# Late stage of a diffusion-transformer layer: four PSUM places for the out tiles, the first tiles interleaved by k, the sums of squares added behind the norm's steps

## What is computed

```python
merged = sigmoid(g_dn) * (y_dn @ w_branch_dn) + sigmoid(g_at) * (y_at @ w_branch_attn)
x = x + g_a_x * (merged @ w_out)
h = modulate(rms_norm(x, norm_ffn), sh_f_x, sc_f_x)
u = dwconv_centred(h @ ffn_up, ffn_conv) + ffn_conv_b      # 1024 -> 2 * 2816 channels
x = x + g_f_x * ((silu(u_gate) * u_val) @ ffn_down)
```

## Time and profile before

| | |
|---|---|
| median of 3 runs | 2613.94 us (2612.71 to 2618.61) |
| the profiled execution: its time | 2618.86 us |
| its span, first to last instruction | 2617.1 us |
| instructions in the profile | 40,299 |
| `late_stage` from its first out tile to its third up tile | 1773.8 to 1899.6 us |

### The profile page before, as it was taken

One profiled execution on the slowest core, in us unless ns is written; L12 is line 12 of the kernel. 1 busy time (PEld: TensorE's weight loads), 2 busy tenths in 40 slices (PEclk: granted clock), 3 DMA queues, 4 the chain that ended last, 5 costly groups with the idle time before them and its releaser, 6 DMA issues. The chain is left out here.

```text
span 2617.1 us, 40299 instructions
## 1 busy us (share of the span) xinstructions
PE 2504.8 (96%) x16246; PEld 2088.3 (80%) x16246; DVE 1393.0 (53%) x2110; ACT 811.8 (31%) x1745; POOL 858.4 (33%) x580
## 2 busy tenths in 40 slices
PE   5999999999999999999999989999899999997999
PEld 4768887887888888888888877887688888886887
DVE  6783665213456565565656564256865555555342
ACT  4222554101264554635454463101211111112010
POOL 1443652332324132323324131335433333322121
PEclk9999999999899999999999999999999999998999
DMA  7231322222000010101001011224411111113442
GB/s 271 72 81 53 122 109 90 97 73 81 17 18 25 18 33 9 34 9 42 25 18 33 2 42 57 97 97 126 158 57 49 49 49 49 49 36 102 140 129 90
DMA packets 52646, 177.01 MB, mean 68 GB/s; under 512 B 5360, under 2 KB 14960, under 8 KB 51184
## 3 DMA queue, kind: packets, MB, share of 16 engines
q1 hardware_dynamic: 50160, 170.24, 20.0%
q10 hardware_dynamic: 2304, 4.20, 0.4%
HBM read 148.20 MB, written 20.97 MB: 65 GB/s over the span
## 5 line engine op out<-in xcount | busy, mean ns | idle before, releaser
L201 PE MATMUL late_ps<-h_hi,late_w_hi 128*128 128x512 f32 x784 | 306.4, 391 | 5.8 <-ACTq L127 3.2
L203 PE MATMUL late_ps<-h_hi,late_w_lo 128*128 128x512 f32 x784 | 306.1, 390 | 0.0
L202 PE MATMUL late_ps<-h_lo,late_w_hi 128*128 128x512 f32 x784 | 306.0, 390 | 0.0
L1403 PE MATMUL late_ps<-h_hi,dn_w_hi 128*128 128x512 f32 (+1 forms) x640 | 248.2, 388 | 5.6 <-issue 5.6
L1403 PE MATMUL late_ps<-h_lo,dn_w_hi 128*128 128x512 f32 (+1 forms) x640 | 252.2, 394 | 0.0
L1403 PE MATMUL late_ps<-h_hi,dn_w_lo 128*128 128x512 f32 (+1 forms) x640 | 249.9, 390 | 0.0
L184 POOL CAST late_w_hi<-late_w_raw 128x1024 fp32r<-128x1024 f32 x76 | 79.2, 1042 | 505.9 <-issue 376.2
L191 POOL TENSOR_TENSOR late_w_lo<-late_w_raw,late_w_hi 128x1024 fp32r<-128x1024 f32 x76 | 204.0, 2685 | 6.1
L2444 DVE SCALAR_TENSOR_TENSOR ffn_u<-ffn_pad,vectors,ffn_u 128x1024 f32<-128x1024 f32 x88 | 194.5, 2210 | 3.1
L201 PEld LDWEIGHTS late_ps<-h_hi,late_w_hi 128*128 128x128 f32 x784 | 147.7, 188 | 37.3 <-issue 6.7
L202 PEld LDWEIGHTS late_ps<-h_lo,late_w_hi 128*128 128x128 f32 x784 | 147.6, 188 | 30.8 <-issue 0.2
(11 more groups left out here) (360 smaller groups left out, 6027.3 us busy)
## 6 DMA issues: line engine op xcount, KB each, us to landing
late_w_raw<-in_w_up SPq DMA_DIRECT2D x44, 512.0 KB, 3.5
down_w_raw<-in_w_down SPq DMA_DIRECT2D x32, 704.0 KB, 4.3
late_w_ada<-in_w_ada SPq DMA_DIRECT2D x8, 2048.0 KB, 8.4
dn_w_raw<-in_w_dn SPq DMA_DIRECT2D x32, 512.0 KB, 3.9
w_ada<-in_w_ada SPq DMA_DIRECT2D x8, 1024.0 KB, 11.1
at_w_raw<-in_w_mg_at SPq DMA_DIRECT2D x16, 512.0 KB, 4.0
late_w_raw<-in_w_mg_dn SPq DMA_DIRECT2D x16, 512.0 KB, 3.7
late_w_raw<-in_w_out SPq DMA_DIRECT2D x16, 512.0 KB, 3.8
```

The source lines that it names most:

```text
L201: pe.matmul(out, self.hi[j][:, k, :], xh, start=(k == 0), stop=False)
L202: pe.matmul(out, self.hi[j][:, k, :], xl, start=False, stop=False)
L203: mm = pe.matmul(out, self.lo[j][:, k, :], xh, start=False, stop=(k == self.kt - 1))
L1403: mm = pe.matmul(bank[at_bank(s)][:, 0:n], wt[:, k, :], x[:, k, t0:t0 + n], start=(rest == 0), stop=(rest == GROUP_MM - 1))
```

## The change

Four things change in `late_stage`.

1. Out tiles use the four halves of `ps[0]` and `ps[1]`, and tile q waits for the residual of tile q - 4 (`x1_made(q - 3)`).
2. Out tiles 0 and 1 are interleaved: k = 0 to 6 of tile 0, k = 0 to 6 of tile 1, then k = 7 of tile 0, k = 7 of tile 1. All k-steps of both wait for `merged_lo` of their k.
3. The second token half of the first two up tiles is interleaved by k: for each k, three matmuls of tile 0 and three of tile 1. The wait for the last residual is taken once, ahead of the loop.
4. The adding of the squares leaves `residual(q)` and becomes `added(q)`. For q up to 9 it stands behind the next tile's residual; for q = 10 to 13 behind the two `scaled` and two `low` steps of that turn; for q = 14 and 15 where it was.

No instruction is added or removed, and no size changes.

```diff
--- before.py
+++ after.py
@@ -2188,7 +2188,7 @@
 
         def x1_place(q):
 
-            return ps[0][:, half(q % 2)]
+            return ps[q % 4 // 2][:, half(q % 2)]
 
         with nc.Block() as block:
             @block.sync
@@ -2253,13 +2253,27 @@
                     pe.matmul(ps[3][:, half(b)], mats[:, C_ONE, :], rstd[:, half(b)], start=True, stop=True).then_inc(ss_done, 1)
 
                 sig_ready.wait(pe, KT)
-                for q in range(2 * KT):
+
+                def out_part(q, k0, k1):
+
                     i = LATE_OUT + q
-                    pe.wait_ge(w.split, i + 1)
-                    x1_made.wait(pe, q - 1)
-                    mm = w.product(pe, x1_place(q), i % 2, m_hi, m_lo, q // KT * HALF, HALF,
-                                   parts=m_lo_made if q == 0 else None)
-                    mm.then_inc(w.used.sem, 1)
+                    if k0 == 0:
+                        pe.wait_ge(w.split, i + 1)
+                        x1_made.wait(pe, q - 3)
+                    tk, o = half(q // KT), x1_place(q)
+                    for k in range(k0, k1):
+                        if q < 2:
+                            pe.wait_ge(m_lo_made, k + 1)
+                        pe.matmul(o, w.hi[i % 2][:, k, :], m_hi[:, k, tk], start=(k == 0), stop=False)
+                        pe.matmul(o, w.hi[i % 2][:, k, :], m_lo[:, k, tk], start=False, stop=False)
+                        mm = pe.matmul(o, w.lo[i % 2][:, k, :], m_hi[:, k, tk], start=False, stop=(k == KT - 1))
+                    if k1 == KT:
+                        mm.then_inc(w.used.sem, 1)
+                for k0, k1 in ((0, KT - 1), (KT - 1, KT)):
+                    for q in range(2):
+                        out_part(q, k0, k1)
+                for q in range(2, 2 * KT):
+                    out_part(q, 0, KT)
                     if q == KT + 1:
                         squares(0)
 
@@ -2273,15 +2287,16 @@
                     up_half(t, 0)
                     if t == 0:
                         squares(1)
-                for t in range(2):
-                    for k in range(KT):
-                        h_lo_made.wait(pe, KT + k + 1)
-                        x1_made.wait(pe, 2 * KT)
+                x1_made.wait(pe, 2 * KT)
+                for k in range(KT):
+                    h_lo_made.wait(pe, KT + k + 1)
+                    for t in range(2):
                         o = ps[t][:, half(1)]
                         pe.matmul(o, w.hi[t][:, k, :], h_hi[:, k, half(1)], start=(k == 0), stop=False)
                         pe.matmul(o, w.hi[t][:, k, :], h_lo[:, k, half(1)], start=False, stop=False)
                         mm = pe.matmul(o, w.lo[t][:, k, :], h_hi[:, k, half(1)], start=False, stop=(k == KT - 1))
-                    mm.then_inc(w.used.sem, 1)
+                        if k == KT - 1:
+                            mm.then_inc(w.used.sem, 1)
                 pe.wait_ge(std_made, 2)
 
                 def up_tile(t, place):
@@ -2382,6 +2397,10 @@
                     dve.wait_ge(x_res_in[q % 2], q // 2 * 16 + 16)
                     dve.scalar_tensor_tensor(out=x1[:, t, half(b)], in0=x1_place(q), scalar=core.gate_mix[:, t:t + 1],
                                              in1=x_in[:, q % 2, :], op0=ALU.mult, op1=ALU.add).then_inc(x1_made.sem, 1)
+
+                def added(q):
+
+                    t, b = q % KT, q // KT
                     sq_made.wait(dve, q + 1)
                     acc = rstd[:, half(b)]
                     if t == 0:
@@ -2410,6 +2429,9 @@
                                              op1=ALU.subtract).then_inc(h_lo_made.sem, 1)
                 for q in range(KT + 2):
                     residual(q)
+                    if q:
+                        added(q - 1)
+                added(KT + 1)
                 root(0)
                 for q in range(KT + 2, 2 * KT):
                     residual(q)
@@ -2417,6 +2439,7 @@
                         scaled(0, k)
                     for k in steps_of(q):
                         low(0, k)
+                    added(q)
                 root(1)
                 scaled(1, 0)
                 for k in range(KT):
```

## The result

The changed kernel takes 2620.58 us (median of 22 runs, 2617.32 to 2626.89) beside 2616.01 us of the kernel before on the same chips: 1.0018 times the time of before, 95% interval 1.0013 to 1.0024. By that ratio it is 4.7 us slower, where the forecast was 1.6 us slower. The time lies 1.1 us above the forecast's range (2610.7 to 2619.5), though its 0.18% are within the 0.2% that the forecast called no change; the upper end of the interval is not. The forecast counted from the 2613.94 us of three runs of the kernel before, and its median is 2.1 us higher over more runs, so of the 5.1 us between forecast and result 2.1 are the starting point, and 3.0 are what the change cost beyond its forecast.

What follows compares the result with a forecast made beforehand. TensorE, busy 96% of the span, was taken as the bound, with only 11.7 us of late-stage waits to win. Terms +0.5 + 2.1 - 1.0 = +1.6 us on 2613.94 gave 2615.5 us, range 2610.7 to 2619.5.

Steps and rivals of the forecast that it cites:

- Part 1: Out tiles 0 and 1 interleaved: `merged_lo` wait becomes about 3.2 us for POOL; tile 2 starts 0.5 to 0.6 us later.
- about 0.1 for restarting: At tile 2's start behind the wait for POOL: PE's restart adds about 0.1 us.
- Parts 2 and 3: Four PSUM places, and DVE from residual 9 on: one 6.0 us wait, first up tile starts +0.5 us, at about 1871.2.
- the waits for squares: DVE's turns q = 10 to 13: four waits of 0.70 us for the square go, -2.8 us.
- POOL's split: Ahead of residual 14: all six weight splits now lie before it and hold DVE, +2.4 us.
- The clock: Behind the 6.0 us wait ahead of the first up tile: PE falls to 1.2 GHz, +2.1 us, bounds 0 and 5.1.
- Part 4: Up tiles interleaved: small waits give way to about 3 us for POOL; up tile 2 starts 1.0 us earlier.
- from there to residual 10: Addition of square 8 behind residual 9 lengthens POOL's `lo` and delays the addition of 9: +0.3 us.
- DVE loses all that it gained: Rival, DVE's turns ahead of the first up tile: +3.3 + 2.1 - 1.0 = +4.4 us, 2618.3 us; chance 0.09.

Runs made afterwards that it cites:

- the experiment with short `lo`: Changed kernel with POOL's `lo` for out tiles 11 to 15 and up tiles 0 and 1 cut to one of 8 blocks: 2610.97 us, ratio to before 0.9984.
- the fillers: Changed kernel plus matmuls of no use in PE's three long waits (12, 26 and 12): 2616.01 us, ratio to before 1.0003.

## Why the prediction was off

**Part 1** was right in its working: the wait for POOL was forecast at about 3.2 us and is 3.0, tile 2 starts 0.43 us later where 0.5 to 0.6 was forecast. **The step that failed** is the next one: the sum took "about 0.1 for restarting" and no clock. The clock fell there, 1.4 us in the profile.

**Parts 2 and 3** named the right mechanism and had two of their terms wrong in size. There is one wait ahead of the first up tile, forecast 6.0 and measured 6.7 us, and the experiment with short `lo` shows that the bound was named rightly. That tile's start was forecast at 97.4 us after out tile 0 and is 99.4. Most of the 2.0 is part 1's fall of the clock. The rest lies in the turns of DVE: residual 10 to the end of residual 14 takes 32.5 us, before 32.0, where -2.8 for the waits for squares and +2.4 for POOL's split had given -0.4. Both terms missed the same way: the squares moved with two places make these turns 2.45 us shorter (29.5), and four places then make them 3.0 longer. The moved additions are on two SBUF inputs as well, and two of them now meet POOL's `lo` in the changed kernel and take 2.88 us each, where before the four took 1.3 to 1.6.

**The clock** behind the long wait fell as forecast; its price was 1.3 us in place of 2.1.

**Part 4** was right in its order: from the first to the third up tile it takes 29.1 us, 28.9 before; with 1.3 for the clock in between that is -1.1, forecast -1.0. Again the sum left out the fall behind the wait: 1.7 us behind up tile 2's start.

The whole difference of the two profiles, beside the terms of the forecast (clock: 24 matmuls behind the wait, beside the same 24 of the kernel before; its step behind a wait is in them):

| term | forecast, us | measured, us |
|---|---|---|
| start of tile 2 | +0.6 | +0.43 |
| clock behind tile 2's start | 0 | +1.44 |
| from there to residual 10 | +0.3 | +0.07 |
| residual 10 to the end of residual 14 | -2.8 + 2.4 | +0.54 |
| clock behind the first up tile's start | +2.1 | +1.31 |
| first to third up tile without the clock | -1.0 | -1.08 |
| clock behind the third up tile's start | 0 | +1.70 |
| sum | +1.6 | +4.41 |

So the term "The clock" was mis-sized: taken once, at 2.1 us, where it stands three times, 1.44 + 1.31 + 1.70 = 4.45 in the profile; the fillers gave 4.0 of it back. That is 2.35 us of the 2.8 that the sum missed, the turns of DVE are 0.9, and the small terms give 0.5 back. The rival "DVE loses all that it gained" has the measured number, +4.4, by luck: it puts 2.8 us more on DVE and one fall of the clock, where DVE took 0.9 more and the clock 2.35.

The forecast priced the wait of 6 us and never asked the same of the two new waits for POOL. It also said that the kernel before shows nothing between 2.7 and 13.1 us of idling. That was misread. The profile of before has a wait of 3.15 us ahead of the matmul at 1619.78, and the clock fell behind it (waits from 1500 on, then the stretch behind the wait, columns as in the earlier trace rows):

```profile
PE late_ps L201 <- ACTq L127: 3.2, 1, 3.2
```

```profile
1620.00:1623.50 3.50, 3.50 (x10) 2.69 (x10) 0.00 (x0) 3.15 (x3) 3.14 (x2) 0.52 0.57 181
```

It has one of 5.56 us too, ahead of 627.7, and the granted clock is 0.52 from 627 to 634. Either would have asked for a fall behind the new waits as a term of the sum.

What the fall of the clock hangs on stays open. From out tile 0 to the down projection, in all ten profiles, the clock fell behind each wait of 3.0 us (6 of 6) and each of 6.7 us or more (3 of 3), and behind one of the ten waits of 2.4 to 2.7 us. Ahead of out tile 0, in the same profiles, the length of a wait does not decide alone: a wait of 3.15 us is followed by a fall in four of the ten profiles (clock 1.00 from 1618 to 1622 in the changed kernel), and a wait of 2.4 us near 445, behind small matmuls of 128 columns, goes with a fall in all ten. So a wait in one place is followed by a fall in some executions and not in others, and each kernel has one profile. By the Trainium skill ("TensorE: Matmul & The Clock Gate", Part 1) the throttled clock is the default and activity releases it; the trace agrees: the clock fell in waits, and the steps of 0.43 us behind tile 2's start end at 1787.14, 2.7 us after PE works again. What a fall costs behind a wait is 1.3 to 3.0 us in these profiles.

## What to carry to other kernels

Before filling a wait by interleaving two tiles, ask what starts at the end of the first: a later end delays the next weights, and the work that stood behind it was their cover. Interleave only as far as the wait needs. Before giving TensorE more PSUM places, ask whether the engine that frees them keeps up on average; here it was held by GpSimd, and PE running ahead only gathered two short waits into one long one. And give each new wait of TensorE of some 3 us a price for the fall of the clock behind it, each one by itself, with a chance read from waits of that length in the same profile, wherever in the kernel they stand.

## What the runs showed of the hardware

- Behind out tile 0, a wait of 3.0 us was followed by a fall to 1.2 GHz in 6 of 6 cases, one of 2.4 to 2.7 us in 1 of 10. Elsewhere in the same profiles a wait of 3.15 us was followed by one in 4 of 10, and one of 2.4 us behind small matmuls in 10 of 10. A fall behind a wait of 3.0 us cost 1.4 to 3.0 us, measured over the 24 matmuls behind it.
- Useless matmuls in the three waits kept the clock at 1.00, and were worth 4.0 us for 50 matmuls.
- When a DVE instruction with two SBUF inputs was pending as POOL's cast ended, it ended first, and POOL's next instruction took 2.7 in place of 2.4 us. In the changed kernel the cast ends at 1792.66, the addition that started at 1792.16 ends at 1793.20, and `lo` takes 2.72 us from 1792.74.
